# A two-layer encoder on one core: the state-space loop with its angle tables built through PSUM, its tiles in six places, and GpSimd's order by pairs

## The reference, cut to what matters

```python
for l in range(2):                                   # SEQ 256, D 1024
    proj = rmsnorm(x, norm_mix[l]) @ w_in[l]         # q | k | v | u, 512 columns each
    attn = dilated_attention_mixture(q, k, v, rel_bias)          # 8 heads x 64
    # bidirectional S5: 32 groups x 64 complex states, two directions
    lam_bar = exp(lam * step);  b_bar = (lam_bar - 1) / lam * b
    for direction in (forward, backward):
        states = scan(state = lam_bar * state + b_bar @ u)       # over the 256 positions
        y += Re(c @ states)
    y = gelu(y + d_skip * u);  ab = y @ w_glu[l];  ssm = ab[:512] * sigmoid(ab[512:])
    x = x + concat(rmsnorm(attn), rmsnorm(ssm)) @ w_out[l]
    x = x + peer(rmsnorm(x, norm_ffn[l]))            # 16384 single-neuron experts, top 16 of 8 heads
out = rmsnorm(x, norm_final)
```

## Time and profile before

| what | value |
|---|---|
| median of 3 runs | 2240.35 us (2234.82 to 2241.8) |
| the profiled execution: its own time, its span | 2243.86 us, 2242.0 us |
| PE, DVE, ACT, POOL busy, of the span | 92%, 70%, 46%, 31% |
| granted clock of TensorE, mean | 0.968 |
| POOL's loop, layer 0 (first `drives` to last `turn_out`) | 39.27 to 204.13 us |
| POOL's loop, layer 1 | 1148.70 to 1316.63 us |

### The profile page before, as it was taken

The page is one execution under the profiler, slowest core; times in us unless marked ns, Lnnn a source line. Parts: engine busy times, 40 slices in busy tenths (PEclk is TensorE's granted clock), DMA queues, the critical chain, the costliest instruction groups (busy, mean ns, idle before and its releaser), DMA issues.

```text
span 2242.0 us, 38988 instructions
## 1 busy us (share of the span) xinstructions
PE 2069.4 (92%) x12654; PEld 1758.2 (78%) x12654; DVE 1566.5 (70%) x2948; ACT 1036.5 (46%) x1763; POOL 696.5 (31%) x548
## 2 busy tenths in 40 slices
PE   6878899977999999999988888999779999999997
PEld 4554599976888999999865546998778889999996
DVE  6875499877677666666687845998767766666665
ACT  3433354478334444444343333455863354444443
POOL 2995176755000000000048852676640000000000
PEclk9998999999999999999989989999999999999999
DMA  4213255310558555555322123543015565555553
GB/s 175 71 52 144 94 170 183 123 48 23 185 195 296 187 186 186 186 186 186 129 91 85 64 115 116 190 162 114 29 57 191 192 226 187 187 187 186 186 186 115
DMA packets 90109, 329.33 MB, mean 147 GB/s; under 512 B 10355, under 2 KB 14579, under 8 KB 87964
## 3 DMA queue, kind: packets, MB, share of 16 engines
q1 hardware_dynamic: 89996, 328.13, 43.3%
q10 hardware_dynamic: 16, 0.02, 0.0%
HBM read 324.94 MB, written 3.16 MB: 146 GB/s over the span
## 4 chain that ended last, share of the span: by engine, by line
PE 59%; DVE 14%; POOL 10%; issue 8%; DVEq 5%; ACT 2%; POOLq 1%; DMA 1%; ACTq 0%; SPq 0%
PE ps L751 32%; PE ps L730 19%; POOL arena L1590 5%; DVE arena L1183 5%; POOL v_raw L1590 2%; PE ps L702 2%; DVEq L1465 2%; POOL u_raw L1590 2%; DVE arena L1432 1%; DVE arena L1425 1%; DVE arena L1426 1%; PE ps L693 1%; PE ps L813 1%; PE ps L595 1%; PE ps L560 1%
## 5 line engine op out<-in xcount | busy, mean ns | idle before, releaser
L751 PE MATMUL ps<-v_hl,w_hl 128*128 128x512 f32 x3072 | 732.7, 393 | 6.5 <-DVE v_hl L1183 6.5
L751 PEld LDWEIGHTS ps<-v_hl,w_hl 128*128 128x128 f32 x3072 | 568.2, 189 | 126.3 <-DVE v_hl L1183 10.1
L730 PEld LDWEIGHTS ps<-h_hl,u_hl 128*128 128x128 f32 x4800 | 600.0, 192 | 12.8
L730 PE MATMUL ps<-h_hl,u_hl 128*128 128x256 f32 x4800 | 609.6, 284 | 0.0
L1590 POOL TENSOR_TENSOR arena<-arena 128x256 f32<-128x256 f32 (+1 forms) x240 | 217.8, 938 | 662.7 <-DVE arena L1183 634.7
L1036 ACT ACTIVATE v_hl<-v_raw 128x1024 fp32r<-128x1024 f32 x208 | 220.8, 1062 | 306.7 <-PE ps L751 285.1
L1183 DVE TENSOR_TENSOR u_hl<-u_raw,u_hl 128x1024 fp32r<-128x1024 f32 x148 | 181.3, 1225 | 199.8 <-ACT u_hl L998 196.8
L998 ACT ACTIVATE u_hl<-u_raw 128x1024 fp32r<-128x1024 f32 x144 | 152.9, 1062 | 247.3 <-PE ps L730 245.0
L1183 DVE TENSOR_TENSOR v_hl<-v_raw,v_hl 128x1024 fp32r<-128x1024 f32 x208 | 253.9, 1220 | 12.4 <-ACT v_hl L1036 12.2
L730 PE MATMUL ps<-h_hl,v_hl 128*128 128x256 f32 x1344 | 171.5, 285 | 0.1
L1183 DVE TENSOR_TENSOR arena<-arena 128x512 f32<-128x512 f32 (+4 forms) x164 | 158.7, 983 | 10.9 <-issue 4.2
(11 more groups left out here) (167 smaller groups left out, 2404.3 us busy)
## 6 DMA issues: line engine op xcount, KB each, us to landing
u_raw<-in_expert_u SPq DMA_DIRECT2D x208, 512.0 KB, 3.3
v_raw<-in_expert_v SPq DMA_DIRECT2D x208, 512.0 KB, 3.3
v_raw<-in_expert_u SPq DMA_DIRECT2D x48, 512.0 KB, 4.5
u_raw<-in_expert_v SPq DMA_DIRECT2D x48, 512.0 KB, 3.2
arena<-in_w_in SPq DMA_DIRECT2D x16, 512.0 KB, 3.6
arena<-in_w_in SPq DMA_DIRECT2D x8, 1024.0 KB, 5.3
arena<-in_ssm_b SPq DMA_DIRECT2D x16, 512.0 KB, 4.3
arena<-in_w_out SPq DMA_DIRECT2D x2, 4096.0 KB, 12.2
```

Of the source, the lines that this page charges most:

```text
L730: m = pe.matmul(ps[:, bank, o:o + S], hl[:, wp, k, :], h_hl[:, hp_, k, :], start=(k == 0 and j == 0), stop=(k == DC - 1 and j == 2))
L751: m = pe.matmul(ps[:, 2 * a + half, :], w_hl[s][:, wp, a * P:(a + 1) * P], v_hl[s][:, vp, half * 512:(half + 1) * 512], start=(first and j ...
```

## The change

The angle table's outer sum goes to PSUM (bank 0, which q and k leave), before the wait for the table's old place, and the rounding and the difference read it there; from pair 3 on the second row of 16 comes from PSUM too, where one copy per layer has put it. A tile's turned input, drive and state share one place, of six (`SLOTS`): `turn_in` writes it, `drives` and `scan` work on it in place, `turn_out` reads it. The wait for a free place moves from `scan` to `turn_in`, three pairs back. u, q, k and v are all projected into bank 1, so q waits for `copy_u` and v for `copy_qk`. POOL does both tiles' `drives` of the next pair, then both `turn_out`, and a third of `c_terms`, spread over pairs 0, 1 and 2. On DVE `y_sum` and `attn_out` trade places and `y_sum` moves to pair 1; on ACT `gelu_y` goes behind `exps`. SBUF's layout keeps its size.

```diff
@@ SBUF
-        turn_f = take(2 * 2 * S)
-        turn = turn_f.rearrange("p (s r t) -> p s r t", s=2, r=2)
+        turn_f = take(SLOTS * 2 * S)
+        state = turn_f.rearrange("p (s r t) -> p s r t", s=SLOTS, r=2)
         turn2 = take(2 * 2 * S).rearrange("p (s r t) -> p s r t", s=2, r=2)
-        drive = take(2 * 2 * S).rearrange("p (s r t) -> p s r t", s=2, r=2)
-        state = take(2 * 2 * S).rearrange("p (s r t) -> p s r t", s=2, r=2)
@@ PE: project, c_pair, projections
                     if lo == 0 and kind == 0:
                         pe.wait_ge(s_w_qk, 16 * (it + 1))
-                        pe.wait_ge(s_qk_sb, 1 + it)
+                        pe.wait_ge(s_u_sb, it + 1)
                     if lo == 0 and kind == 2:
                         pe.wait_ge(s_w_v, 16 * (it + 1))
-                        pe.wait_ge(s_u_sb, it + 1)
+                        pe.wait_ge(s_qk_sb, 1 + it + 1)
...
-                        bank, o = {3: (1, S), 0: (0, 0), 1: (0, S)}[kind]
+                        o = {3: S, 0: 0, 1: S}[kind]
                         for k in range(lo, hi):
-                            m = pe.matmul(ps[:, bank, o:o + S], w_slot[:, kind, k, :], hT[:, k, :],
+                            m = pe.matmul(ps[:, 1, o:o + S], w_slot[:, kind, k, :], hT[:, k, :],
...
-                    for kind, lo, hi in {(0, False): ((3, 0, 4),), (0, True): ((3, 4, 8),), (1, False): ((0, 0, 3),),
+                    for kind, lo, hi in {(0, False): (), (0, True): ((3, 0, 8),), (1, False): ((0, 0, 3),),
                                          (1, True): ((0, 3, 8),), (2, False): ((1, 0, 3),), (2, True): ((1, 3, 8),),
-                                         (3, False): ((2, 0, 1),), (3, True): ((2, 1, 2),)}[s, late]:
+                                         (3, False): (), (3, True): ((2, 0, 2),)}[s, late]:
@@ ACT: the loop over q
                     angles(q * PAIRS + 3)
-                    if q:
-                        gelu_y(q - 1)
                     if more:
                         copy_u(q + 1)
                     exps(q, 0)
                     exps(q, 1)
+                    if q:
+                        gelu_y(q - 1)
@@ DVE: block_turns, turn_in, scan, the loop
+                    if g < FIRST_PAIRS:
+                        b_some = some[:, :, 16:32]
+                    else:
+                        o = n_all + (g - FIRST_PAIRS) * 32
+                        b_some = ps[:, MAG_BANK, o:o + 32].rearrange("p (n b) -> p n b", n=2)
+                    b_part = b_some.unsqueeze(2).broadcast_to(shape)
+                    turns_ps = ps[:, TURN_BANK, :]
+                    dve.drain()
+                    tt(turns_ps.rearrange("p (n a b) -> p n a b", n=2, a=16), a_part, b_part, ALU.add)
                     dve.drain()
                     if q:
-                        done = 2 + l * NQ * NT + 2 * (g - PAIRS + 1)
+                        done = SLOTS + l * NQ * NT + 2 * (g - PAIRS + 1)
                         dve.wait_ge(s_outc, done)
                         dve.wait_ge(s_outs, done)
-                    tt(tab[:, 0, tiles, :].rearrange("p n (a b) -> p n a b", a=16), a_part, b_part, ALU.add)
-                    dve.drain()
-                    dve.tensor_scalar(tab[:, 1, tiles, :], tab[:, 0, tiles, :], ROUND, ROUND, ALU.add, ALU.subtract)
-                    dve.drain()
-                    tt(tab[:, 0, tiles, :], tab[:, 0, tiles, :], tab[:, 1, tiles, :], ALU.subtract)\
-                        .then_inc(s_turns, 1)
+                    turns_ps = turns_ps.rearrange("p (n t) -> p n t", n=2)
+                    dve.tensor_scalar(tab[:, 1, tiles, :], turns_ps, ROUND, ROUND, ALU.add, ALU.subtract)
+                    dve.drain()
+                    tt(tab[:, 0, tiles, :], turns_ps, tab[:, 1, tiles, :], ALU.subtract).then_inc(s_turns, 1)
...
                     dve.wait_ge(s_drive, it * NT + n + 1)
-                    src = ps[:, 5 + s, :].rearrange("p (r t) -> p r t", r=2)
-                    tt(turn[:, s, :, :], src, two(1, n), ALU.mult)
-                    tt(turn2[:, s, :, :], src, two(0, n), ALU.mult).then_inc(s_pp, 1)
-
-                def scan(q, n):
-                    s, it = n % 2, l * NQ + q
-                    dve.wait_ge(s_drive, 2 + it * NT + n + 1)
                     dve.wait_ge(s_outc, it * NT + n + 1)
                     dve.wait_ge(s_outs, it * NT + n + 1)
+                    src = ps[:, 5 + s, :].rearrange("p (r t) -> p r t", r=2)
+                    tt(state[:, (q * NT + n) % SLOTS, :, :], src, two(1, n), ALU.mult)
+                    tt(turn2[:, s, :, :], src, two(0, n), ALU.mult).then_inc(s_pp, 1)
+
+                def scan(q, n):
+                    it, z = l * NQ + q, state[:, (q * NT + n) % SLOTS, :, :]
+                    dve.wait_ge(s_drive, 2 + it * NT + n + 1)
                     r_all = ps[:, MAG_BANK, q * NT + n:q * NT + n + 1].broadcast_to([P, S])
                     for r in range(2):
-                        dve.tensor_tensor_scan(state[:, s, r, :], r_all, drive[:, s, r, :], 0.0,
+                        dve.tensor_tensor_scan(z[:, r, :], r_all, z[:, r, :], 0.0,
...
-                    if q and s == 0:
-                        attn_out(q - 1)
+                    if g == 0:
+                        dve.tensor_copy(ps[:, MAG_BANK, n_all:n_all + (NQ * NT - 2 * FIRST_PAIRS) * 16]
+                                        .rearrange("p (n b) -> p n b", b=16), angle[:, 2 * FIRST_PAIRS:, 16:32])
+                    if q and s == 1:
+                        y_sum(q - 1)
                     scan(q, 2 * s)
                     if s == 1:
                         row_max(q, 0)
                     scan(q, 2 * s + 1)
                     if q and s == 0:
-                        y_sum(q - 1)
+                        attn_out(q - 1)
@@ POOL: c_terms in three parts, drives, turn_out, the loop
                 def drives(q, n):
-                    s, it = n % 2, l * NQ + q
+                    s, it, z = n % 2, l * NQ + q, state[:, (q * NT + n) % SLOTS, :, :]
                     pool.wait_ge(s_pp, 2 + it * NT + n + 1)
-
-                    pool.wait_ge(s_state, 2 * (it * NT + n) + 2)
-                    tt(drive[:, s, 0, :], turn[:, s, 0, :], turn2[:, s, 1, :], ALU.add)
-                    tt(drive[:, s, 1, :], turn[:, s, 1, :], turn2[:, s, 0, :], ALU.subtract).then_inc(s_drive, 1)
+                    tt(z[:, 0, :], z[:, 0, :], turn2[:, s, 1, :], ALU.add)
+                    tt(z[:, 1, :], z[:, 1, :], turn2[:, s, 0, :], ALU.subtract).then_inc(s_drive, 1)
...
                 for g in range(NQ * PAIRS):
                     q, s = divmod(g, PAIRS)
+                    if g + 1 < NQ * PAIRS:
+                        for j in range(2):
+                            drives((g + 1) // PAIRS, (g + 1) % PAIRS * 2 + j)
                     for j in range(2):
-                        if g + 1 < NQ * PAIRS:
-                            drives((g + 1) // PAIRS, (g + 1) % PAIRS * 2 + j)
                         turn_out(q, 2 * s + j)
-                    if s == 1 and q + 1 < NQ:
-                        c_terms(q + 1)
+                    if s < 3 and q + 1 < NQ:
+                        c_terms(q + 1, s)
```

More of the change, by code:

```diff
@@ L57 @@
 HOT = 4
+SLOTS = 6
 BATCHES = 4
@@ L211, in encoder @@
         MAG_BANK = 3
+        TURN_BANK = 0
+        FIRST_PAIRS = 3
         ps = ctx.enter_context(nc.psum_tensor("ps", [P, 8, 512], F32))
@@ L588, in c_pair @@
                         pe.wait_ge(s_c, 1 + it + 1)
-                    pe.wait_ge(s_outc, 2 + it * NT + 2 * p + 2)
-                    pe.wait_ge(s_outs, 2 + it * NT + 2 * p + 2)
+                    pe.wait_ge(s_outc, SLOTS + it * NT + 2 * p + 2)
+                    pe.wait_ge(s_outs, SLOTS + it * NT + 2 * p + 2)
                     for j, (kind, part) in enumerate(((0, 0), (1, 1), (2, 0), (2, 1))):
@@ L908, in copy_qk @@
                     act.wait_ge(s_proj, 3 + 3 * (l * NQ + q) + 2)
-                    act.activation(qT, ps[:, 0, 0:S], ACT.Copy, scale=HD ** -0.5)
-                    act.activation(kT, ps[:, 0, S:2 * S], ACT.Copy).then_inc(s_qk_sb, 1)
+                    act.activation(qT, ps[:, 1, 0:S], ACT.Copy, scale=HD ** -0.5)
+                    act.activation(kT, ps[:, 1, S:2 * S], ACT.Copy).then_inc(s_qk_sb, 1)
                 def copy_v(q):
@@ L1170, in _ @@
             dve.sem_inc(s_gates, 4)
-            for counter in (s_u_mm, s_v_mm, s_gelu, s_pp, s_drive, s_outc, s_outs):
+            for counter in (s_u_mm, s_v_mm, s_gelu, s_pp, s_drive):
                 dve.sem_inc(counter, 2)
+            for counter in (s_outc, s_outs):
+                dve.sem_inc(counter, SLOTS)
             dve.sem_inc(s_proj, 3)
-            dve.sem_inc(s_state, 4)
             dve.sem_inc(s_y, 4)
@@ L1324, in _ @@
                 dve.memset(fence[:, 2:3], 0.0)
-                for g in range(3):
+                for g in range(FIRST_PAIRS):
                     block_turns(g)
@@ L1602, in _, with c_terms @@
```

(43 more changed lines are left out.)

5 lines of the change are left out of this document (2 added, 3 removed).

## The result

The changed kernel takes **2188.1 us** (median; 2185.8 to 2188.5) against 2240.3 before: ratio 0.977, 95% interval 0.975 to 0.979, or 52 us less.

The account below looks back on a forecast made before the run. GpSimd was taken to pace the mixers' loops. The 22.9 and 25.9 us to be had there, less 3.0 for TensorE and 0.75 ahead of the loop per layer, gave 41.3 us off: 2200 us, range 2189 to 2226.

Parts of the forecast that it names:

- The bound: In the two mixers GpSimd sets the pace, with loops of 164.9 and 167.9 us and little room beside it.
- Contention: In the mixers' loops, `block_turns`' two-SBUF-operand instructions on VectorE slow GpSimd; 12.3 and 11.0 us per layer would go.
- Waits for scans: GpSimd's waits in the loops, 10.6 and 14.9 us, would go because the wait for a place moves to `turn_in`.
- TensorE, 3.0 us per layer: In three quarters per layer TensorE's work makes each 36.5 us instead of GpSimd's 35.5, giving back 3.0 us.
- GpSimd's own sum, 142.0 per layer: GpSimd's loop without contention or waits: sixteen pairs, 124.8 us, plus four `c_terms`, 17.2 us, gives 142.0.
- the low end of the range: Kernel time of 2189 us: all that is to be had in the loops, 48.8 us, and a run's few us.
- The head, 0.75 per layer: Ahead of the loop, the first three tables' roundings read PSUM at 0.68 instead of 0.43 us, 0.75 us later.
- The sum: Over both mixer layers, gains of 19.2 and 22.2 us, together 41.3, with the median forecast at 2200 us.
- 1 (TensorE paces): In the loops TensorE becomes the pacer and is often late, quarters 39.1 us; kernel 2215 us, chance 0.20.
- 2: The loop is a ring across engines whose pace stays, contention's gain turning into waiting; kernel 2240 us, chance 0.07.
- rival 3: In the loops, pauses put TensorE's work at 1.2 GHz, making quarters 46.0 us; kernel slower, 2254 us, chance 0.07.
- 4: In the loops PSUM operands don't spare GpSimd, so only its waits go, 18 us; kernel 2222 us, chance 0.06.

Follow-up runs that it names:

- e1: The kernel before with only the angle tables built through PSUM and all projections in one bank; 2209.2 us, ratio 0.987.
- e2: The changed kernel with the three angle-table instructions of the kernel before, built in SBUF; 2215.8 us, ratio 0.990.
- e9: The kernel before with tables through PSUM, one projection bank and TensorE's, ScalarE's and VectorE's new orders, without the six places or GpSimd's new order; 2203.0 us.
- e10: The changed kernel with GpSimd's old order, tile by tile and `c_terms` in one block; 2188.4 us, ratio 0.977.
- e5: The changed kernel with four places for a tile in the loop instead of six; 2191.9 us, ratio 0.979.
- e8: The changed kernel with `y_sum` and `attn_out` back in VectorE's old places; 2189.7 us, ratio 0.978.
- e7: The changed kernel with u's projection done twice in three quarters, 3.7 us more TensorE work in each; 2196.0 us, ratio 0.981.
- e12: The changed kernel with `c_terms` moved from GpSimd to VectorE, its factors and one product of each sum in PSUM; 2183.2 us, ratio 0.974.
- e6: The changed kernel with the tables' sum reading two SBUF inputs again, its output staying in PSUM; 2200.1 us, ratio 0.983.
- e11: The changed kernel with a shorter way to the loop: two tables and the first tiles' turns before C's coefficients; 2183.3 us, ratio 0.974.

## Why the prediction was wrong, point by point

- **The bound: right.** GpSimd set the pace, and the experiments' loops follow its work and its waits. Of the signs that the prediction named, most came: GpSimd's means, the tables at 692 to 696 ns, a clock of 0.94, no waits for scans. The loop of "about 146 us" (its own terms give 142.0 + 3.0 = 145.0) and the quarter of 36 to 37 did not.
- **Contention: right in mechanism and instructions, and in price within 1.3 us a layer** (12.3 and 11.0 us by the prediction's terms, 13.6 and 12.3 by the busy time). `block_turns` alone made it (e1, e2); GpSimd's means went to the clean rows (714 and 1284 ns, against 723 and 1268), and its busy time of 151.8 became 138.2.
- **Waits for scans: they went, for the reason given.** The places do it (e9 against e10, e5). That two of the orders beside them bring nothing (e8, e10) the prediction had said of GpSimd's, not of `y_sum`.
- **TensorE, 3.0 us per layer: the step that failed, for the forecast.** It was "I put the quarter at 36.5 us, 0.5 over PE's busy time". The quarter took 35.0, GpSimd's own pace. The 36.0 of the earlier trace rows was busy time at a granted clock of 0.96, as the quarter held a stretch at 1.2 GHz, behind a wait for `turn_in`. That wait, from the timeline of TensorE before, and the window of the stretch:

```profile
119.31 1.49 PE L577 MATMUL ps<-v_raw,arena 32*128 32x256 f32 x8 [3.98 <-DVE arena L1183]
119.95:123.37 3.42, 3.42 (x20) 1.32 (x18) 3.18 (x4) 0.00 (x0) 3.29 (x5) 0.50 0.01 2
```

 At the full clock the same work would take half of these 3.4 us: 36.0 - 1.7 = 34.3 (an estimate from the two rows). Measured in the changed kernel, with these waits gone and the clock at 1.00, it is 33.4 to 34.0. Work was taken from a row whose duration came in part from the very waits that the change removes. And e7 shows that TensorE could have been 2.1 us late once a layer without harm. Two layers: 6.0 us of the miss.
- **GpSimd's own sum, 142.0 per layer: 1.9 too high,** 3.8 us in all, **and the step that failed for the low end of the range.** A pair is 7.7 us, not 7.8 (e12, where POOL does nothing but pairs: 123.2 / 16), and `c_terms` 4.2, not 4.3. The prediction let a gap ahead of each pair use up what neighbours overlap by; there is none: of POOL's 1.9 us idle 1.8 are around `c_terms`' drains. The low end took "all that is to be had" as 48.8, worked out from the 142.0, and left two or three us below it for a run; the TensorE term is not in it. The loops gave 52.5.
- **The head, 0.75 per layer: right.** The rounding from PSUM takes 692 ns against 427. From the start of the first table to the copy behind the third VectorE takes 6.8 us instead of 6.0. POOL starts 1.4 us later in layer 0, where the first projection also started 0.9 later, and 0.7 later against the first projection in layer 1. The 692 agrees with the rule of the Trainium skill ("VectorE: DVE Perf Modes", Why PSUM operands drop a tier) that float32 in PSUM loses the doubled rate.
- **The sum** was 41.3 us. With the two terms put right it is 41.3 + 6.0 + 3.8 = 51.1, against 52 between the medians. That the rest is so small is partly luck: the sum was made from the profiled execution, and between the two profiled executions lie 55.3 us. Of the 4.3 that are missing there, 2.8 are the two forms of the first part of the experts' stage (last section); the others are small differences between the other stretches outside the loops.
- **Rivals.** 1 (TensorE paces) is wrong for this change; with 3.7 us more work in a quarter it would have been right (e7), and one step further it is VectorE that paces, just ahead of TensorE (e12). 2, 3 and 4 fall; rival 3's clock went the other way, from 0.87 to 0.94 over the loop. TensorE did pause ahead of `c_pair` in both quarters shown above, for 1.6 and 1.0 us, and the clock was 1.00 throughout.

## What to carry to other kernels

When GpSimd paces a stage, look at what VectorE runs beside it: moving one operand of each of the tables' instructions to PSUM took 13 us a layer off GpSimd's busy time (e1), and made VectorE's own instructions faster too, though the rounding lost its doubled rate. When several engines are busy for nearly the whole of a stage, don't take an engine's busy time from a row at a reduced clock as its work: scale it to the clock that it will have once its waits are gone, and ask how much lateness the buffers can carry. To name the pacer, go by who waits for whom and not by the busy shares: in e12 VectorE paced with 94% busy, its own gaps making up the rest, beside a TensorE with 99%. For a wait between two tiles' places, go through the handing-over tile by tile before pricing it.

## What the runs showed of the hardware

- A VectorE sum with two SBUF inputs held GpSimd up by 0.41 us although its output went to PSUM (e6).
- In this kernel one sum from PSUM and SBUF beside a busy GpSimd takes VectorE 684 to 696 ns, and the rounding from PSUM 692; with SBUF alone they took 1139 and 1099.
- The first part of the experts' stage, where no instruction was changed, came in two lengths, 179.8 or 178.4 us from the first expert's matmul to the gates, in one and the same execution of e1 even, with VectorE's busy time at 163 or 140 us. Windows of e1, layer 0 and layer 1:

```profile
254.82:434.63 179.81, 178.26 (x1400) 172.95 (x1399) 163.45 (x488) 91.17 (x177) 125.62 (x51) 1.00 0.50 165
1347.12:1525.54 178.42, 178.01 (x1401) 172.91 (x1399) 140.42 (x488) 91.20 (x177) 124.26 (x51) 1.00 0.51 168
```

 TensorE is busy throughout in both, so 23 us of VectorE's time go with no more than 1.4 of the stage. Of the 26 such stretches in the 13 profiled executions 6 are long: both of before, and one each of e1, e2, e5 and e11. In before's, the largest group of VectorE's sums from SBUF to SBUF has a mean of 1333 ns against 940 in the changed kernel's short one, and GpSimd's 128x1024 sums 2600 and 2528 against 2465 and 2475. That looks like the mixer's contention again, by how the two engines' instructions happen to lie beside each other; what chooses was not tried. Before has the long form in both layers, the changed kernel the short one: 2.8 us between the two spans.
